# A hybrid decoder step: the samples' delta rule on VectorE's fused products, and the first 256 tokens as two 256-column products copied by ACT

## The reference

```python
q, k = l2norm(q), l2norm(k)              # of one sample, 128 each
S   = S * exp(g)                         # S: 128 x 128 (k x v), one of 8 samples
u   = (v - S.T @ k) * beta
S   = S + outer(k, u)                    # returned as delta_sample
o   = S.T @ (q * 128 ** -0.5)
out = o * rsqrt(mean(o * o) + EPS) * onorm_w    # then times silu(z)
```

## Time and profile before

| | |
|---|---|
| median of 3 runs | 1199.55 us (1198.0 to 1202.51) |
| profiled execution | 1204.32 us, its span 1202.5 us |
| granted TensorE clock, mean | 0.992 |
| PE busy | 1165.9 us, 97% |
| PEld busy | 1087.4 us, 90% |
| DVE busy | 801.4 us, 67% |
| ACT busy | 475.1 us, 40% |
| POOL busy | 307.2 us, 26% |
| DMA | 164.18 MB, mean 137 GB/s |

### The profile page before, as it was taken

The page is one execution under the profiler, slowest core; times in us unless marked ns, Lnnn a source line. Parts: engine busy times, 40 slices in busy tenths (PEclk is TensorE's granted clock), DMA queues, the critical chain, the costliest instruction groups (busy, mean ns, idle before and its releaser), DMA issues. The chain is left out here.

```text
span 1202.5 us, 24731 instructions
## 1 busy us (share of the span) xinstructions
PE 1165.9 (97%) x8401; PEld 1087.4 (90%) x8401; DVE 801.4 (67%) x1987; ACT 475.1 (40%) x1216; POOL 307.2 (26%) x275
## 2 busy tenths in 40 slices
PE   5999999999999999999999999999999979999997
PEld 4899989998999899989988999899999979999996
DVE  5586567666766786777766766777776756565544
ACT  6453335434533444344434433453345335331211
POOL 0224112411242134122311241223122312222211
PEclk9999999999999999999999999999999999999999
DMA  7332455254525452635263525352535373423263
GB/s 249 93 98 73 145 158 162 72 165 147 168 64 177 136 162 62 203 110 166 67 193 108 168 66 194 116 161 81 182 111 168 93 251 129 150 88 101 73 212 143
DMA packets 83354, 164.18 MB, mean 137 GB/s; under 512 B 12801, under 2 KB 22882, under 8 KB 81698
## 3 DMA queue, kind: packets, MB, share of 16 engines
q1 hardware_dynamic: 81966, 161.47, 42.5%
q10 hardware_dynamic: 1312, 1.59, 0.5%
HBM read 144.78 MB, written 17.37 MB: 135 GB/s over the span
## 5 line engine op out<-in xcount | busy, mean ns | idle before, releaser
L643 PE MATMUL PJ<-h,w_hi 128*128 128x512 f32 x1110 | 419.3, 414 | 0.0
L1995 POOL TENSOR_TENSOR w_lo<-w_raw,w_hi 128x512 fp32r<-128x512 f32 x160 | 216.2, 1352 | 758.5 <-ACT w_hi L1035 758.1
L639 PE MATMUL PJ<-h,w_hi 128*128 128x264 f32 (+1 forms) x1216 | 358.0, 294 | 0.0
L640 PE MATMUL PJ<-h,w_hi 128*128 128x264 f32 (+1 forms) x1216 | 345.7, 284 | 0.0
L641 PE MATMUL PJ<-h,w_lo 128*128 128x264 f32 (+1 forms) x1216 | 345.4, 284 | 0.0
L644 PE MATMUL PJ<-h,w_lo 128*128 128x256 f32 x1110 | 311.3, 280 | 0.0
L643 PEld LDWEIGHTS PJ<-h,w_hi 128*128 128x128 f32 x1110 | 209.2, 188 | 42.8 <-DVE w_lo L1397 1.4
L640 PEld LDWEIGHTS PJ<-h,w_hi 128*128 128x128 f32 x1216 | 230.4, 189 | 2.2
L1035 ACT ACTIVATE w_hi<-w_raw 128x512 fp32r<-128x512 f32 x320 | 196.5, 623 | 86.4 <-PE PJ L641 79.1
L639 PEld LDWEIGHTS PJ<-h,w_hi 128*128 128x128 f32 x1216 | 230.0, 189 | 0.3
L641 PEld LDWEIGHTS PJ<-h,w_lo 128*128 128x128 f32 x1216 | 229.0, 188 | 0.0
(11 more groups left out here) (333 smaller groups left out, 1705.8 us busy)
## 6 DMA issues: line engine op xcount, KB each, us to landing
w_raw<-in_w_in SPq DMA_DIRECT2D x256, 256.0 KB, 2.7
w_raw<-in_w_out SPq DMA_DIRECT2D x64, 256.0 KB, 3.0
kvq<-in_cache_win_k SPq DMA_DIRECT2D x24, 512.0 KB, 5.0
kvq<-in_cache_win_v SPq DMA_DIRECT2D x24, 512.0 KB, 4.8
mem<-scratch_p SPq DMA_DIRECT2D x24, 512.0 KB, 5.7
out<-memx SPq DMA_DIRECT2D x16, 260.0 KB, 4.0
mem<-in_x_prompt SPq DMA_DIRECT2D x4, 1024.0 KB, 10.1
S<-in_state_delta SPq DMA_DIRECT2D x8, 512.0 KB, 5.8
```

The lines of the kernel that those rows point to most:

```text
L639: pe.matmul(ps, wh, h_hi[:, k, tok], start=k == 0, stop=False)
L640: pe.matmul(ps, wh, h_lo[:, k, tok], start=False, stop=False)
L643: pe.matmul(both, wh, h2[:, :, k, tok], start=k == 0, stop=False)
L1995: pool.tensor_tensor(w_lo[:, par, 4 * q:4 * q + 4, :], w_raw[:, q, :, :], w_hi[:, par, 4 * q:4 * q + 4, :].bitcast(F32), ALU.subtract).the ...
```

## The change

1. In the in-projection, half 0 is now always three products of 256 columns (as half 1 has three of 264), and ACT copies it out at segment 5, with the guards that stood before `half_out`. The semaphore `proj_half` is gone; only the out-projection keeps the 512-column form.
2. The samples' delta rule works on a state laid out [v index, sample, k index]. k and q are transposed to rows by VectorE (a 32 x 32 block transpose), written to DRAM in four small DMAs each and read back to all 128 partitions (512 KB each, `k_rows` and `q_rows`). S k and S q are then fused multiply-and-sum instructions on VectorE, one a sample, and the update is one `scalar_tensor_tensor` a sample. PE keeps two products of ones. POOL still scales the state and no longer expands anything.
3. The load of keys(0) moves from SP's step 51 to 52, in front of the read-back of q for the samples' attention, and the value products (L1843 before) start one step later.

```diff
-                wide = half == 0 and not (isinstance(T, int) and T < 2)
+                wide = half == 0 and out
...
@@ PE, delta_decode @@
-                yield from idle(36)
+                yield from idle(35)
                 pe.wait_ge(s["dkq"], h + 1)
-                pe.wait_ge(s["S0_in"], 16 * h + 16)
...
-                pe.matmul(MD[:, 1, 0:24], ones[:], dd[:, 2:5, :].rearrange("p a b -> p (a b)"), start=True, stop=True)
-                for b in range(NB):
-                    last = pe.matmul(MD[:, 1, 32 + 2 * b:34 + 2 * b], S0[:, b, :], dd[:, 0:2, b], start=True,
-                                     stop=True)
...
-                    pe.matmul(MD[:, 1, :], kvr_all[:, 0, :], vexp_all, start=True,
-                              stop=True).then_inc(s["d_outer"], 1)
+                pe.matmul(MD[:, 1, 0:16], ones[:], dd[:, 2:4, :].rearrange("p a b -> p (a b)"), start=True,
+                          stop=True).then_inc(s["d_sum"], 1)
+                yield from idle(14)
                 pe.wait_ge(s["d_vec"], h + 1)
+                pe.matmul(MD[:, 1, 16:24], ones[:], dd[:, 8, :], start=True, stop=True).then_inc(s["d_sq"], 1)
@@ ACT, stretch @@
+                        if seg == 5:
+                            guard(h, j)
+                            copy_out(T, 0, *DST[j])
@@ DVE, stretch @@
-                        if seg == 4 and not (isinstance(h, int) and h == 0 and j == 0):
-                            half_out(h, j)
@@ DVE, fused products and delta_decode from its step 35 on @@
+            def fused(x, rows, out, acc_, per):
+                for b in range(NB):
+                    last = dve.tensor_tensor_reduce(out=out[:, b * P:(b + 1) * P], in0=S0[:, b, :],
+                                                    in1=rows[:, b * P:(b + 1) * P], scale=1.0, scalar=0.0, op0=ALU.mult,
+                                                    op1=ALU.add, accum_out=acc_[:, b:b + 1])
+                    if b + 1 in per:
+                        yield
...
+                dve.wait_ge(s["dk_in"], 16 * h + 16)
+                dve.wait_ge(s["S0_in"], 16 * h + 16)
+                yield from fused(s["d_ks"], k_rows, q_rows, dd[:, 0], (5,))
...
+                dve.wait_ge(s["S0_scaled"], h + 1)
+                for b in range(NB):
+                    last = dve.scalar_tensor_tensor(S0[:, b, :], k_rows[:, b * P:(b + 1) * P], dd[:, 4, b:b + 1],
+                                                    S0[:, b, :], ALU.mult, ALU.add)
+                    if b in (2, 4):
+                        yield
+                last.then_inc(s["d_add"], 1)
+                yield
+                dve.wait_ge(s["d_add"], h + 1)
+                dve.wait_ge(s["dq_in"], 16 * h + 16)
+                yield from fused(None, q_rows, q_rows, dd[:, 1], (3, 5, 6))
@@ SP, delta_decode and decode_keys @@
-                yield from idle(24)
+                yield from idle(16)
+                sp.wait_ge(s["q_row"], 3 * h + 1)
+                rows_to(scratch_dk[h])
+                yield from idle(3)
+                sp.wait_ge(s["qrow_out"], 192 * h + 64)
+                sp.dma_start(k_rows, scratch_dk[h].rearrange("b d -> (b d)").partition_broadcast(P)).then_inc(
+                    s["dk_in"], 16)
...
+                sp.dma_start(q_rows[:], scratch_dq[h].rearrange("b d -> (b d)").partition_broadcast(P)).then_inc(
+                    s["dq_in"], 16)
...
-                yield from idle(51)
+                yield from idle(52)
                 if not first:
                     sp.wait_ge(s["pv_ok"], h)
                 keys(0)
-                yield
-                sp.wait_ge(s["qrow_out"], 64 * h + 64)
+                sp.wait_ge(s["qrow_out"], 192 * h + 192)
@@ POOL, delta_decode @@
                 yield from idle(37)
-                pool.wait_ge(s["d_sum"], h + 1)
+                pool.wait_ge(s["d_ks"], h + 1)
```

More of the change, by code:

```diff
@@ L616, in segment @@
                 if q == 0 and not first:
-                    if half == 1 or out or isinstance(T, int) and T <= 2:
-                        pe.wait_ge(s["proj_sb"], made(T, half) - 2)
-                    else:
-                        pe.wait_ge(s["proj_half"], T - 2)
+                    pe.wait_ge(s["proj_sb"], made(T, half) - 2)
                 tok = TOKENS[half]
@@ L1057, in copy_out @@
             def copy_out(T, half, dst, off=0):
-                late = not (isinstance(T, int) and T < 2)
                 act.wait_ge(s["proj_ps"], made(T, half))
-                if late:
-                    act.wait_ge(s["proj_half"], T - 1)
                 o = off + half * SPLIT
@@ L1442, in _ @@
             dve.memset(gt, 0.0)
-            dve.memset(rt_all[:].bitcast(F32), 0.0)
             dve.memset(ones[:], 1.0).then_inc(s["memset_ok"], 1)
@@ L1539, in own_a @@
                 dve.wait_ge(s["q_ok"], h + 1)
-                if not first:
-                    dve.wait_ge(s["qrow_out"], 64 * h)
+                dve.wait_ge(s["qrow_out"], 192 * h + 128)
                 dve.transpose(qrow[:], xa[:, TT - 32:TT]).then_inc(s["q_row"], 1)
@@ L1740, in delta_decode @@
             def delta_decode(h):
+                first = isinstance(h, int) and h == 0
                 kd, qd = xk[:, TP:TT], cq[:, TP:TT]
-                yield from idle(33)
+                yield from idle(15)
+                dve.wait_ge(s["kv_silu"], 2 * h + 1)
+                if not first:
+                    dve.wait_ge(s["qrow_out"], 192 * h)
+                dve.transpose(qrow[:], xk[:, TT - 32:TT]).then_inc(s["q_row"], 1)
+                yield from idle(18)
                 dve.wait_ge(s["q_silu"], h + 1)
-                dve.wait_ge(s["kv_silu"], 2 * h + 2)
@@ L1789, in delta_decode @@
                                          ALU.mult).then_inc(s["gated_bd"], 1)
-                for n in range(2):
-                    yield from idle(n + 1)
-                    dve.wait_ge(s["d_outer"], 2 * h + n + 1)
-                    dve.wait_ge(s["S0_scaled"], h + 1)
-                    st = S0[:, 4 * n:4 * n + 4, :]
-                    dve.tensor_tensor(st, st, MD[:, 1, :].rearrange("p (b e) -> p b e", b=4), ALU.add).then_inc(
-                        s["d_add"], 1)
             def bt_s(n):
@@ L1818, in key_block, with attn_decode @@
                 last.then_inc(s["red"], 1)
-            def attn_decode(hh, late=0, gap=31, each=2):
+            def attn_decode(hh, late=0, gap=32, each=2):
                 yield from idle(13 + late)
```

200 lines of the change are left out of this document (79 added, 121 removed).

## The result

The changed kernel takes 1203.92 us (median of 6 runs, 1202.59 to 1206.36), the kernel before 1199.0 beside it: a ratio of 1.0039, 95% interval 1.0022 to 1.0056. I had forecast 1185 (1177 to 1195), so it lies outside my range and on the other side of no change. Within my own bound of 0.5% it is "the same", to which I gave 0.09; the interval says that it is a little slower.

What follows compares the result with a forecast made beforehand. TensorE, busy 1165.9 of 1202.5 us, was taken as the bound. 1204.3 − 24.8 + 2.4 + 3.5 + 5 = 1190.4 us; that −13.9 laid on the median 1199.55 gave 1185.6, stated as 1185 (1177 to 1195).

Steps and rivals of the forecast that it cites:

- the same: Outcome for the whole kernel: a time between 1193.5 and 1205.5 us, not told from no change; chance 0.09.
- The work taken off TensorE: Samples' delta rule, eight heads: 24.8 us leave TensorE, two products with ones add 2.4; net −22.4 us (−20 to −24).
- The products: In-projection half 0: 1008 more products, +2.5 to +5 ns a k-step, +3.5 us taken (+2.5 to +5).
- The copy by ACT: Emptying PJ for half 0: ACT rises 3 us a head, VectorE sheds 5.5; costed at nothing.
- the new waits: TensorE stalls at step 51 (0.3 us) and after q's read-back (0.4 us) per head; +5 us, ends 0 and +12.
- The read-back of q: Decode attention: keys(0) ahead adds 1.4 us against 1.08 us of slack, so 0.3 to 0.5 us of stall a head.
- nothing that stands out: TensorE's waits inside the head loop before: 2.4 us in three for VectorE's gate product, one of 1.8 us.
- my rival: VectorE's new two-operand blocks stretched beside GpSimd: 1 to 1.5 us a head stay, 1189 to 1193 us; chance 0.13.
- The slower rival: Steps 35 to 47: late k or q rows delay VectorE and the level products; at 3.2 us a head 1206; chance 0.07.
- my own test lines: Next profile: TensorE busy down 17 to 21 us, VectorE 64 to 68%; wrong if loop waits for VectorE exceed 12 us.
- the rival on weight loads: TensorE's weight loads become the bound: 1008 more less some 90, 9310 × 0.129 = 1205 us; chance 0.01.

Runs made afterwards that it cites:

- three products alone: Kernel before with half 0 of the in-projection as three 256-column products, VectorE still emptying the bank by a same-size instruction: 1202.02 us, ratio 1.0025.
- the split alone: Kernel before with half 0 of the in-projection as three 256-column products, copied out by ACT with its guards: 1207.70 us, ratio 1.0069.
- third block behind gB: Changed kernel, keys(0) still late, with VectorE's eight keys(2) products whole in the head's last step, after the gate product: 1192.89 us, ratio 0.9952.
- late keys and values: Kernel before with only keys(0) loaded at SP's step 52 ahead of q's read-back and value products one step later: 1220.80 us, ratio 1.0195.
- delta rule: Kernel before with only the samples' state update and reads moved to VectorE; half 0, keys(0) and value products as before: 1192.14 us, ratio 0.9950.
- delta rule and split: Changed kernel with keys(0) at SP's step 51 again and the value products one step earlier: 1191.25 us, ratio 0.9938.
- delta rule and late keys: Changed kernel with half 0's 512-column product and VectorE's half-width sum put back: 1207.10 us, ratio 1.0066.
- the keys back: Changed kernel with keys(0) and value products at their old steps, two VectorE products moved a step: 1189.42 us; with keys(2)'s products after the gate product, 1182.83.

## Why the prediction was wrong

**The work taken off TensorE was right.** All that is not a projection product holds TensorE, from start to start, for 213.2 us before and 189.8 after: −23.4, against my −22.4. The two products of ones hold it for 0.14 us each, as L917 had shown (PE, after):

```profile
336.38 0.29 PE L915 MATMUL MD<-dd,ones 128*128 128x16 f32 x2
336.52 0.37 PE L647 MATMUL PJ<-h,w_hi 128*128 128x264 f32 x1
...
363.19 0.29 PE L919 MATMUL MD<-dd,ones 128*128 128x8 f32 x2
363.33 0.36 PE L647 MATMUL PJ<-h,w_hi 128*128 128x256 f32 x1
```

**The products were right** as a sum: I took +3.5, three products alone measured +2.6. Fifteen k-steps of half 0 after, from these rows, are 5.33 us, 0.355 each, the upper of the two distances in the earlier trace rows:

```profile
302.72 0.28 PE L647 MATMUL PJ<-h,w_hi 128*128 128x256 f32 x1
...
308.05 0.28 PE L647 MATMUL PJ<-h,w_hi 128*128 128x256 f32 x1
```

**The copy by ACT, "I cost this at nothing", was wrong.** With the split alone it cost about 3.7 us: 2.4 for the gate product (4.1 against 1.7) and 1.3 for the late copy in the first head. In the changed kernel ACT's late copies held TensorE for 1.3 us in the first head and 0.8 in the last.

**The step that failed is "the new waits", +5 us with a high end of 12.** By the starts, the waits that are new or longer in the changed kernel add up so: L871 10.0, gB 9.0 − 3.7 = 5.3, L840 3.2 against 0.6, L881 3.0 against 2.0, L812 1.0, ACT's copies 2.1; 2.0 less at the out-projection's start and 1.1 less in the first 35 us: 18.9. The profiled execution of the kernel before has one wait of 2.2 us for gB and 10 us at a granted clock of 0.83 behind it, and its two heads around them take 119.6 and 119.3 us instead of 117.7, 3.5 us in all; it lies 4.8 us above the median of the runs, so I take it that the others do not have this. −23.4 + 2.6 + 18.9 = −1.9, and with those 3.5 us taken out of the base it is +1.6 of the 4.9 measured. The remaining 3 us I can place only in part (half 1's products start 0.5 ns further apart in the changed kernel, 126.07 against 125.55 ns, 1.5 us over some 3070), and the rest stays open.

Inside that term of +5 us, which measured some 19, three things were off.

1. *The read-back of q.* I had the place, the releaser and the slack right and the size wrong. I took 1.4 us for the company of keys(0) against 1.08 us of slack, so 0.3 to 0.5 us a head. The landing grew by 1.9 us (4.8 to 6.7), and the issue itself came 0.64 us later against VectorE, most of it the 0.5 us that the issue of keys(0) takes on SP between the weight load's and q's: VectorE is ready 3.55 us after q's issue, before 4.19. 1.9 + 0.64 − 1.1 is 1.4; measured are 0.94 to 1.61 us a head in the loop. I had read the difference of one load's median and best as the price of company, and left out what SP itself needs. Nor was q "issued alone" before: a weight load of 256 KB goes out 0.52 us ahead of it there too (373.65 in head 3), so its 4.8 us already held some company.
2. *The knock-on.* VectorE, late by q, makes ScalarE late, ScalarE makes GpSimd's weight split late, the weight load waits for that split, and keys(2) stands behind the weight load in SP's order; then VectorE waits for keys(2), gB stands behind it in VectorE's order, and TensorE waits for gB. The sum has no term for any of this. The wait for gB was in the earlier trace rows and I called it nothing that stands out. It was the sign that this hand-over had no slack. The third block behind gB took 11.0 us off the changed kernel.
3. *GpSimd beside VectorE's two-operand instructions.* The mechanism of my rival is in the trace: the updates take 0.536 us in the mean instead of 0.35. Its price on TensorE is about 0.3 us a head (L840), not 1 to 1.5.

**The slower rival had the wrong load.** I looked for it in the delta rule's own rows; the fused products never waited for theirs. The stall was at an older read-back, in front of which the change put a load. Of my own test lines, the one on TensorE's waits for VectorE (over 12 us) is the one that fired; VectorE's share (64%) and the fused products (0.282 us) came as said, TensorE's busy time fell by 13.3 us and not by 17 to 21. In the rival on weight loads the count was off: 160 products a run went away beside the 1008 that came, not "some 90" (8401 to 9249). Nothing hangs on it.

**The parts by themselves**, in us against the base: late keys and values +21.4, split +8.6, delta rule −7.3; delta rule and split −7.8; delta rule and late keys +8.0; all three +4.9. They do not add up (the three alone make +22.7), and no run shows why: the late keys and values cost 21.4 us on the kernel before, 15.3 beside the delta rule and 12.7 beside both. The last two are more than the rest had gained (7.3 and 7.8).

## What to carry to other kernels

Where a change moves a load one place in front of another that an engine already waits for, price it as three things: the issues it adds ahead, the landing with those bytes in flight, and everything on other engines and queues that stands behind the waiting engine's work. A wait of the bottleneck engine that the profile showed only three times, 2.4 us in all, marked a hand-over without slack here, and it grew to 9.0 us once something before it came late. Put instructions that wait for a DMA behind the ones the bottleneck engine needs in the same step: here that order alone was worth 2.3 us on the kernel before, 6.6 with the keys back and 11.0 with them late.

## What the runs showed of the hardware

A 512 KB load issued 0.5 us ahead of a 512 KB read-back, between it and a 256 KB weight load, delayed its landing from 4.8 to 6.7 us (medians of 8); one of 64 KB at the same place still delayed it to 5.7. A VectorE update of 128 columns with two SBUF operands took 1.40 us beside a GpSimd instruction of 1.29 us and 0.35 without; a value product of 384 columns took 1.62 us beside one of 1.27 us and 0.55 without. In the unrolled out-projection of one kernel VectorE stood 3.32 us before an instruction with nothing to wait for, and TensorE with it for 2.7; the kernel before shows such a gap of 4.66 us on ACT near the same place, while TensorE waited for VectorE. The cause of these gaps stays open.
